# Attention of a transformer block: another order of turns, bias rows for each query tile side by side, and the high halves of the gated product on GpSimd

## The chip, the cores and the metric

The kernel runs on one core of a Trainium2 chip. The metric is the device time of one execution in microseconds. The program is one long instruction stream for each of the five engines: TensorE (PE, with its weight loads shown as PEld), VectorE (DVE), ScalarE (ACT), GpSimd (POOL) and SyncE (SP), which here only issues DMAs. The streams wait for each other through semaphores.

## What is computed

Two transformer blocks follow each other on 512 tokens of 1024 values: first an attention with a forget gate and a SwiGLU network, then a gated linear attention and a mixture of 64 experts. The change lies only in the first attention, the "fox" mixer. It has 16 heads of 64 values; 16 meta tokens stand ahead of the 512 real ones, and their outputs aren't needed.

```python
def _fox_attend(q_blk, c_q, pos_q, k, v, c_k, pos_k):
    s = jnp.einsum('bhqd,bhkd->bhqk', q_blk, k).astype(jnp.float32) * (FOX_HEAD_DIM ** -0.5)
    s = s + (c_q[..., :, None] - c_k[..., None, :])
    s = jnp.where(pos_k[None, :] <= pos_q[:, None], s, -jnp.inf)
    p = jax.nn.softmax(s, axis=-1)
    return jnp.einsum('bhqk,bhkd->bhqd', p, v.astype(jnp.float32))
...
    o = o * jax.nn.sigmoid(gate.astype(jnp.float32))
    return (o.astype(h.dtype) @ w_out).astype(h.dtype)
```

The term of the query, c_q, is the same for a whole row and falls out of the softmax. What stays is a bias for each key, -c_k, the same for all queries of a head, and the causal mask.

## The kernel before

Matrix products with weights are made from split values: a number is taken apart into a high half (a cast to fp32r) and a low half (the value minus its high half), and three products are summed. ACT casts the high halves, POOL subtracts to get the low ones.

The attention stage lies at about 215 to 330 us. The heads are taken in 8 pairs, and each pair in T = 4 query tiles of 128 queries. A step s = 4 p + i is query tile i of pair p; it has n = 16 + 128 (i + 1) keys, so 144, 272, 400 and 528. In each step, for both heads e of the pair:

- PE, `scores(s)`: the scores into PSUM, two steps ahead of the rest of its loop.
- DVE, `rowmax(s)`: adds the bias rows to the scores, writes the sum to SBUF (`Pb`, three buffers) and keeps the negated row maximum. Only the last 128 keys of a tile need the causal mask, so the keys are cut: the unmasked ones against the plain rows `cb`, the last 128 against the masked rows `cbm`; keys from 512 on have a cut of their own, since they lie in another PSUM bank. Each cut is two instructions for each head, the sum and the read of its accumulator.
- ACT, `exps(s)`: the exponential in place, and its row sum.
- DVE, `normed_probs(s)`: the reciprocal of the sums, and the product of the probabilities with it.
- PE, `ptrans(s)`: transposes the probabilities 128 columns at a time into two PSUM banks; ACT, `pt_out(s)`: copies them out.
- PE, `pv(p, half)`: the product with the values for query tiles 0 and 1 (half 0) or 2 and 3 (half 1). It starts with the 16 meta keys (tile `PTm`).
- DVE, `gated(p)`: the output of the pair times the gate, into the one buffer `prod_o`. Its high half is `hTh[p]` (`out_high`), its low half `hTl_first[p]` (`out_low`, POOL). `gated(p)` waits until `out_low(p-1)` has read `prod_o`, and `pv(p, 0)` until `gated(p-1)` has read its PSUM bank.

For the next pair POOL scales the queries and keys (`stage(p, 0)`, `stage(p, 1)`), PE transposes them (`qk(p, 0)` and `qk(p, 1)`, both through the one PSUM bank `QB`), and ACT evicts them to `QT` and `KT` (`qk_out`). The second transpose waits for the first eviction, and `scores` of the pair's first step wait for the second.

The bias rows of a pair come by DMA from `c_dram`, copied to all 128 partitions. `decay_rows(p)` issues them from SP; there are two places for them, so those of pair p wait for the last `rowmax` of pair p-2. POOL then makes the masked rows (`masked_rows(p)`), behind the two `stage` of pair p, and `rowmax` of the pair's first step waits for them. Each engine goes through all of this in the order of its written loop; nothing overtakes. At the end of the last pair, PE mixes the first sums of the output projection in (`early_sums`).

Of the kernel before, what the change touches and what calls it, by code (L numbers as in the profile page):

```python
# [48 lines left out]
def program(nc, x, meta_tokens, attn_norm, ffn_norm, final_norm, fox_w_in, fox_b_f, fox_q_norm, fox_k_norm,  # L49
# [32 lines left out]
    with ExitStack() as ctx:  # L82
# [85 lines left out]
        tail = W_SLOTS * 4096  # L168
        CB = L + SEQ - P
        cbs = [arena[:, 3712:3712 + 2 * CB], wring[:, tail:tail + 2 * CB]]  # L170
        cb = [[v[:, e * CB:e * CB + L] for e in range(2)] for v in cbs]
        cbm = [[v[:, e * CB + L:(e + 1) * CB] for e in range(2)] for v in cbs]
        Pb = [[wring[:, 4096 + (2 * i + e) * L:4096 + (2 * i + e + 1) * L] for e in range(2)] for i in range(3)]
# [3 lines left out]
        PT_last = [qkvg[:, :, e * D:e * D + 2 * P] for e in range(2)]  # L177
        at_ptm = at_pt + 2 * SEQ
        PTm = [wring[0:META, at_ptm + i * 4 * P:at_ptm + (i + 1) * 4 * P].rearrange("p (e q) -> p e q", e=2) for i in range(2)]
        assert at_ptm + 8 * P <= W_SLOTS * 4096 + CK_SLOTS * 1024  # L180
        gateT = [xn_t[:, p * SEQ:(p + 1) * SEQ] for p in range(PAIRS)]
# [492 lines left out]
        def _(sp):  # L674
            for t in range(T):
                sp.dma_start(xres[:, t, :], x[0, t * P:(t + 1) * P, :]).then_inc(s_x[t], 16)
            def decay_rows(p):

                if p >= 2:
                    sp.wait_ge(s_mx, 2 * T * (p - 1))  # L680
                for e in range(2):
                    h = 2 * p + e
                    sp.dma_start(cb[p % 2][e], c_dram[h:h + 1, :].to_broadcast([P, L])).then_inc(s_cb[p % 2], 16)

            for w, (slot, dmas, release) in enumerate(tiles):
                name = tile_names[w]
                if name == "g1":
                    sp.wait_ge(s_eD, evacs(unitsB, first_of["cm", 0]))
                    sp.dma_start(c_dram[:, :], cT).then_inc(s_cd, 16)
                elif name == "wo0":  # L690
                    sp.wait_ge(s_mB, first_of["f", 0] + 1)
                    sp.dma_start(gainrow[:, :], final_norm.rearrange("(a n) -> a n", a=1).to_broadcast([P, D])).then_inc(s_row, 16)
                    sp.wait_ge(s_cd, 16)
                    sp.wait_ge(s_hr, 3)
                    decay_rows(0)
                elif name == "wo1":
                    sp.wait_ge(*v1_done)
                    for p in range(1, PAIRS):
                        decay_rows(p)
# [73 lines left out]
        def _(act):  # L773
# [146 lines left out]
            for s in range(NS):  # L920
                p, i = divmod(s, T)
                if s + 1 < NS:
                    exps(s + 1)
                if i == 0 and p + 1 < PAIRS:
                    qk_out(p + 1, 0)
                if i == 1 and p:
                    out_high(p - 1)
                pt_out(s)
                if i == 0 and p + 1 < PAIRS:
                    qk_out(p + 1, 1)  # L930
                if p == PAIRS - 1 and i == 0:
                    high_half(act, attn_end)
                if p == PAIRS - 1 and i == 2:
                    high_half(act, attn_end + 1)
                    high_half(act, attn_end + 2)
            out_high(PAIRS - 1)

# [250 lines left out]
        def _(pe):  # L1188
# [247 lines left out]
            for s in range(NS):  # L1436
# [5 lines left out]
                elif i == 0 and p:  # L1442
                    pv(p - 1, 1)
                if i == 0 and p + 1 < PAIRS:
                    qk(p + 1, 0)
                ptrans(s)
                if i == 0 and p + 1 < PAIRS:
                    qk(p + 1, 1)
                if s >= NS - 2:
# [498 lines left out]
        def _(dve):  # L1948
# [113 lines left out]
            def rowmax(s):  # L2062

                p, i = divmod(s, T)
                n = META + P * (i + 1)
                cuts = ([(512, n)] if n > 512 else []) + [(0, n - P), (n - P, min(n, 512))]
                if i == 0:
                    dve.wait_ge(s_cb[p % 2], 32 * (p // 2 + 1))
                    dve.wait_ge(s_cbm, p + 1)
# [3 lines left out]
                for m, (a, b) in enumerate(cuts):  # L2073
                    for e in range(2):
                        x = 2 * s + e
                        d = P * i + a - (n - P)
                        bias = cb[p % 2][e][:, a:b] if a == 0 or i == T - 1 else cbm[p % 2][e][:, d:d + b - a]
                        last = m == len(cuts) - 1
# [30 lines left out]
            for s in range(NS):  # L2109
# [3 lines left out]
                normed_probs(s)  # L2113
                if i == 0 and p:
                    gated(p - 1)
# [505 lines left out]
        def _(pool):  # L2621
# [61 lines left out]
            def masked_rows(p):  # L2683

                pool.wait_ge(s_cb[p % 2], 32 * (p // 2 + 1))
                for e in range(2):
                    diag = cb[p % 2][e][:, META:L].rearrange("p (t s) -> p t s", t=T)
                    over3 = amask[:, :].unsqueeze(1).to_broadcast([P, T - 1, P])
                    pool.tensor_tensor(cbm[p % 2][e].rearrange("p (t s) -> p t s", t=T - 1), diag[:, 0:T - 1, :], over3, ALU.add)
                    last = pool.tensor_tensor(diag[:, T - 1, :], diag[:, T - 1, :], amask[:, :], ALU.add)  # L2690
                last.then_inc(s_cbm, 1)

            def out_low(p):
                pool.wait_ge(s_ohi, p + 1)
                pool.tensor_tensor(hTl_first[p], prod_o, hTh[p], ALU.subtract).then_inc(s_olo, 1)
# [109 lines left out]
```

## Time and profile before

| | us |
|---|---|
| median of 3 runs | 1462.0 (1460.33 to 1466.8) |
| time of the profiled execution | 1460.39 |
| its span, first to last instruction | 1458.6 |
| PE busy | 1385.2 (95%) |
| DVE busy | 532.5 (37%) |
| ACT busy | 524.5 (36%) |
| POOL busy | 476.3 (33%) |
| mean granted TensorE clock | 0.992 of full speed |

Busy times are over the whole program. Matmuls are pipelined and a row's duration holds the time in the pipeline, so the time from the start of one to the start of the next tells more than the duration of one. Time outside the span is 1.8 us. The attention stage is 115 us of the 1458.6; the last 500 us or so are the experts, whose weights are streamed in at about 419 GB/s.

### The profile page before, as it was taken

How to read it: one execution, taken by the hardware profiler on the slowest of the kernel's cores; microseconds unless marked ns; L12 is line 12 of the kernel's file. 1: busy time of each engine (PE TensorE's matmuls, PEld its weight loads, DVE VectorE, ACT ScalarE, POOL GpSimd, SP SyncE). 2: the span in 40 equal slices, each digit the busy share in tenths (PEclk: the TensorE clock that was granted, in tenths of full speed). 3: DMA queues.
4: the chain of work that ended last, by engine and by line, in shares of the span. 5: the costliest groups of instructions: out<-in, count | busy, mean ns of one | idle time of the engine just before them, and what ended most of it. 6: DMA issues, size and time to landing. Idle time of an engine off the chain costs nothing. (4 is left out here: it accounts for less than half of the span.)

```text
span 1458.6 us, 26900 instructions
## 1 busy us (share of the span) xinstructions
PE 1385.2 (95%) x11180; PEld 1037.7 (71%) x11180; DVE 532.5 (37%) x1383; ACT 524.5 (36%) x1096; POOL 476.3 (33%) x457
## 2 busy tenths in 40 slices
PE   7999998889999999999989999999999999888986
PEld 6788876567788888888867787776666665555553
DVE  3102118761312200212153613355464464444435
ACT  4325438772422222222246532333332222222222
POOL 5334546434544444444455755320000000000000
PEclk9999999999999999999999999999999999999999
DMA  5133221004232223330232131659999999999995
GB/s 187 65 111 115 88 72 47 31 16 147 84 102 71 87 87 115 116 115 15 101 124 97 58 116 59 238 196 390 403 418 420 419 420 419 420 419 420 419 419 208
DMA packets 83899, 286.49 MB, mean 196 GB/s; under 512 B 8764, under 2 KB 31456, under 8 KB 59200
## 3 DMA queue, kind: packets, MB, share of 16 engines
q1 hardware_dynamic: 83376, 283.60, 50.0%
q8 instruction: 91, 1.49, 0.4%
q0 software_dynamic: 288, 1.05, 0.2%
q14 instruction: 32, 0.26, 0.1%
q10 hardware_dynamic: 112, 0.09, 0.0%
HBM read 282.59 MB, written 2.13 MB: 195 GB/s over the span
## 5 line engine op out<-in xcount | busy, mean ns | idle before, releaser
L491 POOL TENSOR_TENSOR wring_halves<-wring,wring_halves 128x512 fp32r<-128x512 f32 x274 | 356.9, 1307 | 376.9 <-ACT wring_halves L486 375.1
L486 ACT CAST wring_halves<-wring 128x512 fp32r<-128x512 f32 x274 | 168.3, 621 | 433.4 <-PE ps L1207 416.6
L1205 PE MATMUL ps<-wring_halves,big_halves 128*128 128x512 f32 x612 | 241.5, 395 | 4.9 <-POOL wring_halves L491 3.8
L1205 PE MATMUL ps<-hT_halves,wring_halves 128*128 128x512 f32 x480 | 187.4, 390 | 2.4 <-DVE big_halves L1964 2.4
L1206 PE MATMUL ps<-big_halves,wring_halves 128*128 128x512 f32 x480 | 186.8, 389 | 0.0
L1207 PE MATMUL ps<-hT_halves,wring_halves 128*128 128x512 f32 x480 | 186.7, 389 | 0.0
L2654 POOL TENSOR_TENSOR rstd<-rstd,half 128x1 f32<-128x1 f32 (+1 forms) x21 | 13.6, 649 | 505.3 <-DVE rstd L2607 476.6
L1207 PE MATMUL ps<-wring_halves,hT_halves 128*128 128x512 f32 x436 | 170.6, 391 | 0.0
L1206 PE MATMUL ps<-wring_halves,hT_halves 128*128 128x512 f32 x436 | 170.6, 391 | 0.0
L1205 PEld LDWEIGHTS ps<-wring_halves,big_halves 128*128 128x128 f32 x612 | 115.4, 189 | 33.4 <-POOL wring_halves L491 7.3
L1725 PE MATMUL ps<-xn,fixed 128*128 128x512 f32 x256 | 120.0, 612 | 0.4 <-DVE fixed L2402 0.4
L1205 PEld LDWEIGHTS ps<-hT_halves,wring_halves 128*128 128x128 f32 x480 | 90.1, 188 | 22.7 <-POOL wring_halves L491 2.9
L1207 PEld LDWEIGHTS ps<-hT_halves,wring_halves 128*128 128x128 f32 x480 | 90.1, 188 | 18.8
L1206 PEld LDWEIGHTS ps<-big_halves,wring_halves 128*128 128x128 f32 x480 | 90.1, 188 | 18.6 <-issue 0.2
L2492 DVE COPY arena<-ps 32x256 f32<-32x256 f32 x128 | 54.3, 424 | 118.5 <-PE ps L1780 113.7
L1207 PEld LDWEIGHTS ps<-wring_halves,hT_halves 128*128 128x128 f32 x436 | 82.3, 189 | 17.5
L1206 PEld LDWEIGHTS ps<-wring_halves,hT_halves 128*128 128x128 f32 x436 | 82.5, 189 | 16.4
L2525 DVE TENSOR_TENSOR xres<-xres,ps 128x512 f32<-128x512 f32 x128 | 82.6, 684 | 21.1 <-PE ps L1806 18.3
L2145 DVE TENSOR_TENSOR arena<-arena,ps 128x512 f32<-128x512 f32 x22 | 15.1, 684 | 195.3 <-ACT arena L955 195.3
L1725 PEld LDWEIGHTS ps<-xn,fixed 128*128 128x128 f32 x256 | 46.5, 192 | 54.2 <-issue 52.4
L1752 PE MATMUL ps<-big,arena 128*32 128x128 f32 x2048 | 65.0, 276 | 10.1 <-DMA big<-in_moe_w_dram 9.6
L1094 ACT COPY arena<-ps 32x256 f32<-32x256 f32 x128 | 46.4, 362 | 62.6 <-PE ps L1780 61.7
(349 smaller groups left out, 1997.5 us busy)
## 6 DMA issues: line engine op xcount, KB each, us to landing
big<-in_moe_w_dram SPq DMA_DIRECT2D x90, 1024.0 KB, 25.4
wring<-in_moe_w_dram SPq DMA_DIRECT2D x70, 1024.0 KB, 25.5
wring<-in_ffn_w_in_dram SPq DMA_DIRECT2D x22, 1024.0 KB, 7.1
hT<-in_moe_w_dram SPq DMA_DIRECT2D x20, 1024.0 KB, 25.3
wring<-in_fox_w_in_dram SPq DMA_DIRECT2D x7, 2048.0 KB, 8.7
wring<-in_gla_w_in_dram SPq DMA_DIRECT2D x6, 2048.0 KB, 7.8
mkv<-in_moe_w_dram SPq DMA_DIRECT2D x12, 1024.0 KB, 26.2
wring<-in_ffn_w_out_dram SPq DMA_DIRECT2D x4, 2048.0 KB, 7.7
```

The source lines that it names most:

```text
L486: act.copy(hi, src).then_inc(s_hi, 1)
L491: pool.tensor_tensor(lo, src, hi, ALU.subtract).then_inc(s_lo, 1)
L1094: last = act.copy(rows[:, n * YG:(n + 1) * YG], bank(6 + j % 2)[n * C:(n + 1) * C, 0:YG])
L1205: pe.matmul(out, lhs[1], rhs[0], start=start, stop=False)
L1206: pe.matmul(out, lhs[0], rhs[1], start=False, stop=False)
L1207: return pe.matmul(out, lhs[0], rhs[0], start=False, stop=stop)
L1725: last = pe.matmul(bank(n), one_hots(g)[1][:, t, :], xn[:, t, n * 512:(n + 1) * 512], start=(t == 0), stop=(t == T - 1))
L1752: last = pe.matmul(o[i * C:(i + 1) * C, 0:2 * HG], xeT[:, k, r * C:(r + 1) * C], w[:, :, i // 2, :, i % 2], start=(k == 0), stop=(k == KD ...
L2145: dve.tensor_tensor(prod[f % 2], sg[f % 2], bank((2 * f + 1) % 8), ALU.mult).then_inc(s_hid, 1)
L2492: last = dve.tensor_copy(rows[:, n * YG:(n + 1) * YG], bank(6 + j % 2)[n * C:(n + 1) * C, 0:YG])
L2525: dve.tensor_tensor(d, d, bank(n), ALU.add).then_inc(done, 1)
L2654: rooted.inc(pool.tensor_tensor(v, v, half[0:v.shape[0], 0:v.shape[1]], ALU.pow))
```

## The change

Four things change.

1. The turns of PE and ACT. In a pair's loop, PE no longer puts the transpose of the next queries ahead of `ptrans` of tile 0 and that of the keys behind it; it puts the queries behind `ptrans` of tile 0 and the keys behind `ptrans` of tile 1. ACT evicts them behind `pt_out` of the same tiles.
2. The gated product of the pair before moves on DVE from behind `normed_probs` of tile 0 to behind that of tile 1, and its high half from ACT to POOL, right ahead of the low half (for the last pair it stays on ACT).
3. The bias rows lie in SBUF once for each query tile, 144 + 272 + 400 + 528 = 1344 columns a head where there were 528 and 384 masked ones. Each is a DMA of its own. POOL adds the mask to the last 128 columns of each in place, and `rowmax` no longer cuts a tile at its last 128 keys.
4. The rows' first place begins lower in `arena`, over values that the projection of the meta tokens reads. So `decay_rows(0)` now waits on SP until that projection is done, ahead of the load of the tile `wo0`, and `PTm` moves to `mkv`.

```diff
-        CB = L + SEQ - P
-        cbs = [arena[:, 3712:3712 + 2 * CB], wring[:, tail:tail + 2 * CB]]
-        cb = [[v[:, e * CB:e * CB + L] for e in range(2)] for v in cbs]
-        cbm = [[v[:, e * CB + L:(e + 1) * CB] for e in range(2)] for v in cbs]
+        KEYS = [META + P * (i + 1) for i in range(T)]
+        CB = sum(KEYS)
+        cbs = [arena[:, 3328:3328 + 2 * CB], wring[:, tail:tail + 2 * CB]]
+        cb = [[[v[:, e * CB + sum(KEYS[:i]):e * CB + sum(KEYS[:i + 1])] for i in range(T)] for e in range(2)] for v in cbs]
...
-        PTm = [wring[0:META, at_ptm + i * 4 * P:at_ptm + (i + 1) * 4 * P].rearrange("p (e q) -> p e q", e=2) for i in range(2)]
+        PTm = [mkv[0:META, i * 4 * P:(i + 1) * 4 * P].rearrange("p (e q) -> p e q", e=2) for i in range(2)]
...
                 for e in range(2):
                     h = 2 * p + e
-                    sp.dma_start(cb[p % 2][e], c_dram[h:h + 1, :].to_broadcast([P, L])).then_inc(s_cb[p % 2], 16)
+                    for i in range(T):
+                        sp.dma_start(cb[p % 2][e][i], c_dram[h:h + 1, 0:KEYS[i]].to_broadcast([P, KEYS[i]])).then_inc(s_cb[p % 2], 16)
...
                     sp.wait_ge(s_hr, 3)
+                    sp.wait_ge(s_mB, unit_of["v", 1, T] + 1)
                     decay_rows(0)
...
@@ ACT @@
                 if s + 1 < NS:
                     exps(s + 1)
-                if i == 0 and p + 1 < PAIRS:
-                    qk_out(p + 1, 0)
-                if i == 1 and p:
-                    out_high(p - 1)
                 pt_out(s)
-                if i == 0 and p + 1 < PAIRS:
-                    qk_out(p + 1, 1)
+                if i < 2 and p + 1 < PAIRS:
+                    qk_out(p + 1, i)
...
+            act.wait_ge(s_ohi, PAIRS - 1)
             out_high(PAIRS - 1)
...
@@ PE @@
-                if i == 0 and p + 1 < PAIRS:
-                    qk(p + 1, 0)
                 ptrans(s)
-                if i == 0 and p + 1 < PAIRS:
-                    qk(p + 1, 1)
+                if i < 2 and p + 1 < PAIRS:
+                    qk(p + 1, i)
...
@@ DVE @@
-                cuts = ([(512, n)] if n > 512 else []) + [(0, n - P), (n - P, min(n, 512))]
+                cuts = ([(512, n)] if n > 512 else []) + [(0, min(n, 512))]
...
-                        bias = cb[p % 2][e][:, a:b] if a == 0 or i == T - 1 else cbm[p % 2][e][:, d:d + b - a]
+                        bias = cb[p % 2][e][i][:, a:b]
...
                 normed_probs(s)
-                if i == 0 and p:
+                if i == 1 and p:
                     gated(p - 1)
...
@@ POOL @@
                 for e in range(2):
-                    diag = cb[p % 2][e][:, META:L].rearrange("p (t s) -> p t s", t=T)
-                    over3 = amask[:, :].unsqueeze(1).to_broadcast([P, T - 1, P])
-                    pool.tensor_tensor(cbm[p % 2][e].rearrange("p (t s) -> p t s", t=T - 1), diag[:, 0:T - 1, :], over3, ALU.add)
-                    last = pool.tensor_tensor(diag[:, T - 1, :], diag[:, T - 1, :], amask[:, :], ALU.add)
+                    for i in range(T):
+                        own = cb[p % 2][e][i][:, KEYS[i] - P:KEYS[i]]
+                        last = pool.tensor_tensor(own, own, amask[:, :], ALU.add)
...
             def out_low(p):
+                if p < PAIRS - 1:
+                    pool.wait_ge(s_prod, p + 1)
+                    pool.tensor_copy(hTh[p], prod_o).then_inc(s_ohi, 1)
```

On PE, in the loop of pair 1, from the end of `pv(0, 1)` (L1402) to the start of `pv(1, 0)` (L1399), the order before is this. L1352 is the transpose of queries or keys, L1380 and L1385 are `ptrans`, L1369 the scores.

```order
L1402 MATMUL ps<-big 64x128 x2
L1352 MATMUL ps<-ident,arena 128x128 x4
L1380 MATMUL ps<-ident,wring 128x128 x2
L1385 MATMUL ps<-ident,wring 16x128 x2
L1352 MATMUL ps<-ident,arena 128x128 x4
L1369 MATMUL ps<-arena 128x272 x2
L1369 MATMUL ps<-arena 128x240 x2
L1380 MATMUL ps<-ident,wring 128x128 x4
L1385 MATMUL ps<-ident,wring 16x128 x2
L1369 MATMUL ps<-arena 128x144 x2
L1399 MATMUL ps<-wring,mkv 64x256 x2
```

The same place of the changed kernel, where every line number on PE is lower by 2:

```order
L1400 MATMUL ps<-big 64x128 x2
L1378 MATMUL ps<-ident,wring 128x128 x2
L1383 MATMUL ps<-ident,wring 16x128 x2
L1350 MATMUL ps<-ident,arena 128x128 x4
L1367 MATMUL ps<-arena 128x272 x2
L1367 MATMUL ps<-arena 128x240 x2
L1378 MATMUL ps<-ident,wring 128x128 x4
L1383 MATMUL ps<-ident,wring 16x128 x2
L1350 MATMUL ps<-ident,arena 128x128 x4
L1367 MATMUL ps<-arena 128x144 x2
L1397 MATMUL ps<-mkv 64x256 x2
```

The first group of L1350 (queries) has gone behind `ptrans` of tile 0, the second (keys) behind the scores of tile 3 and `ptrans` of tile 1, right ahead of the next pair's first scores, which need the evicted keys.

On ACT, in the same stretch, the order before is this. L894 is `exps`, L907 and L908 are `pt_out`, L882 evicts the queries, L886 and L887 the keys, L913 is `out_high`.

```order
L882 ACTIVATE arena<-ps,gcol 128x512
L908 COPY wring<-ps 128x128
L907 COPY wring<-ps 16x2x128
L908 COPY wring<-ps 128x128
L886 COPY arena<-arena 128x16
L887 ACTIVATE arena<-ps,gcol 128x512
L894 ACTIVATE wring,fixed<-wring,fixed 128x400 x2
L913 CAST hT_halves<-wring 128x512
L908 COPY wring<-ps 128x2x128
L907 COPY wring<-ps 16x2x128
L908 COPY wring<-ps 128x2x128
```

And in the changed kernel (line numbers are higher by 1):

```order
L909 COPY wring<-ps 128x128
L908 COPY mkv<-ps 16x2x128
L909 COPY wring<-ps 128x128
L883 ACTIVATE arena<-ps,gcol 128x512
L895 ACTIVATE wring,fixed<-wring,fixed 128x400 x2
L909 COPY wring<-ps 128x2x128
L908 COPY mkv<-ps 16x2x128
L909 COPY wring<-ps 128x2x128
L887 COPY arena<-arena 128x16
L888 ACTIVATE arena<-ps,gcol 128x512
```

The cast has left ACT, and the two evictions stand behind the copies of tiles 0 and 1.

## Rows read from the trace of the kernel before

**Rows 1.** Page, first line: span.

```profile
span 1458.6 us, 26900 instructions
```

**Rows 2.** Windows: us, busy us (x) of PE, PEld, DVE, ACT, POOL; granted clock.

```profile
249.69:257.25 7.56, 7.56 (x70) 5.17 (x70) 5.37 (x24) 5.64 (x18) 6.79 (x13) 1.00 0.21 74
257.25:262.80 5.55, 4.04 (x32) 2.76 (x30) 4.91 (x26) 4.61 (x15) 0.76 (x1) 1.00 0.00 0
...
265.00:267.00 2.00, 2.00 (x13) 1.33 (x11) 1.19 (x2) 1.47 (x5) 1.89 (x5) 0.50 0.41 157
```

**Rows 3.** Timeline, PE and ACT, 257 to 263 us: start, us, instruction [idle before].

```profile
257.25 0.66 PE L1352 MATMUL ps<-ident,arena 128*128 128x128 f32 x4
...
257.64 0.25 PEld L1380 LDWEIGHTS ps<-ident,wring 128*128 128x128 f32 x2
...
257.95 0.69 ACT L882 ACTIVATE arena<-ps,gcol 128x512 f32<-128x512 f32 x1 [1.98 <-PE ps L1352]
...
258.78 0.63 PE L1352 MATMUL ps<-ident,arena 128*128 128x128 f32 x4 [0.43 <-ACT arena L882]
...
259.44 0.20 ACT L886 COPY arena<-arena 128x16 f32<-128x16 f32 x1 [0.25 <-PE ps L1352]
259.55 0.68 ACT L887 ACTIVATE arena<-ps,gcol 128x512 f32<-128x512 f32 x1
...
260.13 0.62 ACT L894 ACTIVATE wring<-wring,fixed 128x400 f32<-128x400 f32 x1
...
261.20 0.52 PE L1369 MATMUL ps<-arena 64*128 64x144 f32 x4
...
261.36 0.61 ACT L913 CAST hT_halves<-wring 128x512 fp32r<-128x512 f32 x1
...
261.87 0.37 ACT L908 COPY wring<-ps 128x256 f32<-128x256 f32 x1
...
262.39 0.36 ACT L908 COPY wring<-ps 128x256 f32<-128x256 f32 x1
...
262.80 0.65 PE L1399 MATMUL ps<-wring,mkv 16*64 16x256 f32 x4 [1.08 <-ACT wring L908]
```

**Rows 4.** Timeline of the last pair, 312 to 318 us.

```profile
312.96 0.69 DVE L2106 TENSOR_TENSOR wring<-ps,xn 128x512 f32<-128x512 f32 x1 [2.67 <-PE ps L1402]
...
313.97 0.61 ACT L486 CAST arena_halves<-wring 128x512 fp32r<-128x512 f32 x1
...
316.14 0.71 PE L1380 MATMUL ps<-ident,wring 128*128 128x128 f32 x4 [1.57 <-DVE wring L2100]
...
317.78 0.65 PE L1399 MATMUL ps<-wring,mkv 16*64 16x256 f32 x4 [0.72 <-ACT wring L908]
```

**Rows 5.** Timeline of the start: SP, POOL, DVE and PE, 215 to 227 us.

```profile
215.40 0.80 SPq L683 DMA_DIRECT2D wring<-c_dram  x2
...
219.60 1.00 POOL L2689 TENSOR_TENSOR wring<-wring,fixed 128x384 f32<-128x384 f32 x1 [9.10 <-DMA wring<-c_dram]
...
224.93 0.16 DVE L2080 CUSTOM_DVE_ANT_0 wring<-ps,wring 128x16 f32<-128x16 f32 x1
...
226.53 1.09 PE L1380 MATMUL ps<-ident,wring 128*128 128x128 f32 x8
```

**Rows 6.** DMA queues, 215 to 224 us: packets, MB, share of 16 engines.

```profile
q1 hardware_dynamic: 288, 0.54, 22.2%
```

**Rows 7.** Groups by shape, 213 to 325 us: POOL (busy us, mean ns | idle).

```profile
L2695 POOL TENSOR_TENSOR big_halves<-wring,hT_halves 128x512 fp32r<-128x512 f32 x7 | 8.9, 1272 | 36.5 <-ACT hT_halves L913 36.5
...
L2689 POOL TENSOR_TENSOR wring<-wring,fixed 128x384 f32<-128x384 f32 x8 | 8.1, 1007 | 9.4 <-DMA wring<-c_dram 9.3
...
L2690 POOL TENSOR_TENSOR wring<-wring,fixed 128x128 f32<-128x128 f32 x8 | 3.7, 461 | 0.0
```

**Rows 8.** Timeline: `normed_probs` of 400 columns, POOL busy, then POOL idle.

```profile
262.79 1.23 DVE L2100 TENSOR_SCALAR wring<-wring,fixed 128x400 f32<-128x400 f32 x2
...
318.54 0.77 DVE L2100 TENSOR_SCALAR wring<-wring,fixed 128x400 f32<-128x400 f32 x2
```

More of the change, by code:

```diff
@@ L177, in program @@
         PT_last = [qkvg[:, :, e * D:e * D + 2 * P] for e in range(2)]
-        at_ptm = at_pt + 2 * SEQ
-        PTm = [wring[0:META, at_ptm + i * 4 * P:at_ptm + (i + 1) * 4 * P].rearrange("p (e q) -> p e q", e=2) for i in range(2)]
-        assert at_ptm + 8 * P <= W_SLOTS * 4096 + CK_SLOTS * 1024
+        PTm = [mkv[0:META, i * 4 * P:(i + 1) * 4 * P].rearrange("p (e q) -> p e q", e=2) for i in range(2)]
+        assert at_pt + 2 * SEQ <= W_SLOTS * 4096 + CK_SLOTS * 1024 and 3328 + 2 * CB <= 6144
         gateT = [xn_t[:, p * SEQ:(p + 1) * SEQ] for p in range(PAIRS)]
@@ L2065, in rowmax @@
                 n = META + P * (i + 1)
-                cuts = ([(512, n)] if n > 512 else []) + [(0, n - P), (n - P, min(n, 512))]
+                cuts = ([(512, n)] if n > 512 else []) + [(0, min(n, 512))]
                 if i == 0:
-                    dve.wait_ge(s_cb[p % 2], 32 * (p // 2 + 1))
+                    dve.wait_ge(s_cb[p % 2], 128 * (p // 2 + 1))
                     dve.wait_ge(s_cbm, p + 1)
@@ L2075, in rowmax @@
                         x = 2 * s + e
-                        d = P * i + a - (n - P)
-                        bias = cb[p % 2][e][:, a:b] if a == 0 or i == T - 1 else cbm[p % 2][e][:, d:d + b - a]
+                        bias = cb[p % 2][e][i][:, a:b]
                         last = m == len(cuts) - 1
@@ L2683, in masked_rows @@
             def masked_rows(p):
-                pool.wait_ge(s_cb[p % 2], 32 * (p // 2 + 1))
+                pool.wait_ge(s_cb[p % 2], 128 * (p // 2 + 1))
                 for e in range(2):
-                    diag = cb[p % 2][e][:, META:L].rearrange("p (t s) -> p t s", t=T)
-                    over3 = amask[:, :].unsqueeze(1).to_broadcast([P, T - 1, P])
-                    pool.tensor_tensor(cbm[p % 2][e].rearrange("p (t s) -> p t s", t=T - 1), diag[:, 0:T - 1, :], over3, ALU.add)
-                    last = pool.tensor_tensor(diag[:, T - 1, :], diag[:, T - 1, :], amask[:, :], ALU.add)
+                    for i in range(T):
+                        own = cb[p % 2][e][i][:, KEYS[i] - P:KEYS[i]]
+                        last = pool.tensor_tensor(own, own, amask[:, :], ALU.add)
                 last.then_inc(s_cbm, 1)
             def out_low(p):
+                if p < PAIRS - 1:
+                    pool.wait_ge(s_prod, p + 1)
+                    pool.tensor_copy(hTh[p], prod_o).then_inc(s_ohi, 1)
                 pool.wait_ge(s_ohi, p + 1)
```

## The prediction

> **What bounds the kernel now.** I read the page first. Of a span of 1458.6 us [rows 1] the change touches only the 115 us of attention; what it wins or loses there moves everything behind it by the same amount, since the projections and the network after it follow on PE at once, and the experts' weight stream starts when its places come free behind them. So the question is what sets the length of one pair of heads.
>
> The windows answer that. A pair is best cut at two points: A runs from the start of pv(p-1, 0) to the end of pv(p-1, 1), B from there to the start of pv(p, 0). In A, 7.56 us, PE is busy for all of it. In B, 5.55 us, PE is busy for 4.04: it idles 1.51 us [rows 2]. ACT is busy for 10.25 of the 13.11 us of the pair, DVE for 10.28, POOL for 7.55. No engine is full over the whole pair; A is PE's, B is a chain. The timeline of B shows the chain [rows 3]: PE turns the queries at 257.25, ACT evicts them at 257.95, PE waits for that (0.43) and turns the keys at 258.78, ACT evicts these at 259.44 to 260.13, makes the exponentials of tile 2 until 261.36, the cast of the gated product until 261.87, the copies of tile 1 until 262.39 + 0.36 = 262.75, and at 262.80 PE starts pv(1, 0), after 1.08 us of idling. 1.08 + 0.43 is the 1.51. DVE's wait of two and more us for the gated product, of which the last pair's is the longest [rows 4], lies beside that chain and is no part of it, except in the last pair, where no queries or keys are turned.
>
> **The chain B after the change.** Each hop has a price in [rows 3].
> - ptrans of tile 0 comes first now: four transposes, 257.25 to 257.64: 0.39.
> - Turning the queries until ACT starts: 257.95 - 257.25 = 0.70.
> - Evicting them, until ACT's next: as for the keys, 260.13 - 259.55 = 0.58.
> - Exponentials of tile 2: 261.36 - 260.13 = 1.23. Their input, rowmax of tile 2, needs scores that PE finished ahead of pv, so it is there.
> - Copies of tile 1, right behind: 0.88 from 261.87 to 262.75, of which about 0.1 overlaps what follows on ACT, as the cast's 0.61 overlaps by 0.10: 0.79. PE has turned tile 1 by then: from the turn of the keys at 258.78 to the end of ptrans of tile 1 at 261.20 it took 2.42, so it is through at 0.39 + 2.42 = 2.81, the exponentials only at 0.39 + 0.70 + 0.58 + 1.23 = 2.90.
> - The keys' eviction, small copy and large: 259.55 + 0.68 - 259.44 = 0.79.
> - From ACT's end to PE: 258.78 - (257.95 + 0.69) = 0.14.
> - The first scores of the next pair, which now stand between: 0.52, and then pv(p, 0) at once.
>
> The sum is 0.39 + 0.70 + 0.58 + 1.23 + 0.79 + 0.79 + 0.14 + 0.52 = 5.14 us, against 5.55. The 0.51 of the cast and the second turn-round of the one bank (0.14 + 0.66 or so) leave the chain; ptrans of tile 0 (0.39) and the scores (0.52) enter it. PE's idle time does not vanish: it stands together now, about 1.1 us, ahead of the scores, waiting for the evicted keys. A doesn't change, since PE is full there. So a whole pair gains 0.41 us, and pairs 1 to 6 give 6 x 0.41 = 2.5 us. Pair 0 gains 0.1 at most: its B was shorter already, having no cast.
>
> **The last pair.** There DVE stood waiting for pv(6, 1) until 312.96 and only then made rowmax of tile 2 and the probabilities of tile 1, for which PE waited 1.57 us [rows 4]. With the gated product behind them, both are ready when PE comes. Then ACT sets the pace: the cast of the weights at 313.97 takes 0.51 to its next, exponentials 1.23, copies 0.88, hop 0.05: pv(7, 0) at 316.64 in place of 317.78 [rows 4]. Gain 1.1 us.
>
> **Moved at no cost.** Merging cuts takes 64 pairs of instructions off DVE; DVE is busy 10.28 of 13.11 us [rows 2] and is not on the chain, so I count nothing for or against it. The gated product moved by a step stays ahead of rowmax of tile 3 and is needed only by pv(p, 0), 5 us later. PTm is as before. On SP, decay_rows(0) and behind it the load of wo0 start later than they did. wo0 is first read in the last pair, at 313.97 [rows 4], some 100 us later. The rows of pair 0 come while the projections' last tile is still being made, and their masks stand on POOL behind that tile's low halves, as before.
>
> **POOL and the rows.** For each pair POOL now makes 8 masks of 128 columns, 8 x 0.46 = 3.7 us, in place of 2 x (1.01 + 0.46) = 2.9 [rows 7], and a cast of 128x512. No row shows a cast on POOL; from below it is 0.46, as the 128 columns take, from above 1.27, as the subtraction of two such inputs takes [rows 7]. I take 1.0, as it has one input and writes as much. POOL's load goes from 7.55 to at most 9.6 us of 12.7: still no bound.
>
> The rows are 8 DMAs of 128 packets, 1.38 MB, in place of 2, 0.54 MB. Before, two landed 219.60 - 215.40 = 4.2 us after the first was issued [rows 5]. The queue moved 288 packets at 22.2% of 16 engines in 9 us, 0.111 us of an engine each [rows 6]; 256 are 1.8 us over 16 engines, which leaves 2.4 us fixed. If bytes set the price, 1.38 MB is 2.55 x 1.8 = 4.5 us; if packets do, 1024 x 0.111 / 16 = 7.1. Issuing eight at 0.4 is 3.2 us and lies beside. So they land 6.9 to 9.5 us after the first issue. From pair 2 on there is room. The rows of pair p+1 are issued when rowmax of tile 3 of pair p-1 is done, 0.2 us (the reciprocal) ahead of normed_probs at 262.79, and needed one pair after the end of that normed_probs [rows 8]: 0.2 + 1.2 + 13.1 = 14.5 us, less 0.4 for the shorter pair. The masks take 3.7, so up to 10.4 us of landing are free.
>
> Pair 1 has no such room. Its rows can't be issued before 215.40, when the projections end. They land at 222.3 to 224.9, are masked at 226.0 to 228.6, and were needed at 224.93 [rows 5]. From there PE started ptrans of tile 3 after 1.6 us, at 226.53 [rows 5]; with two sums in place of four I take 1.2. That comes to 227.2 to 229.8: a loss of 0.7 to 3.3 us, once. I take 1.5, nearer to the price by bytes, as the packets get shorter with the bytes. The Trainium skill (DMA: Bandwidth & Descriptors, Anatomy of one DMA) gives a DMA a fixed part of about 2.0 us and then its bytes at 436 GB/s; by that page the rows would land 2.0 + 3.2 = 5.2 us after the issue, and the loss would be nothing. The rows here moved at 0.54 MB in 1.8 us, which is 300 GB/s, so the row is the slower, and I go by it.
>
> **Sum.** -2.5 (six pairs) - 0.1 - 1.1 (last pair) + 1.5 (rows of pair 1) = -2.2 us. The profiled execution took 1460.4 us, so 1458.2; the median of the runs shown stands 1.6 above it, so I say 1459.8. Ends of this case: the loss 0.7 to 3.3, the chain 0.2 us a pair either way, and stretches at half clock: between 265 and 267 us the granted clock was 0.50 [rows 2], the lower of its two levels, 1.2 of 2.4 GHz, with PE busy before; two us at that level cost about one, and a second such stretch stands a pair later. One or two more or fewer shift the time by 1 to 3 us. So -6 to +2, 1456 to 1464.
>
> **Rivals.**
> 1. PE is fed fully: all 1.51 us of idling go in seven pairs, and 1.1 in the last: -11.7, 1450. It needs the keys' eviction to be ready before PE asks. Against it: ACT's hops in series behind the queries' turn are longer than PE's work there. Chance 0.06.
> 2. Slower: rows land late in every pair. It decides at 10.4 us of landing and 0.4 of slack that DVE has there (1.6 - 1.2). At 14 us each of six pairs would be 3.2 us late, 19 in all, and pair 1 by 7.8 (215.4 + 14 + 3.7 + 1.2 - 226.5): with the gains +23, 1485. For it: 2.5 times the bytes, four times the packets, all reading one row of DRAM. Against: even the price by packets ends at 9.5. Chance 0.06.
> 3. POOL, now busier, slows DVE. Two normed_probs of 400 columns took 1.23 us with POOL busy and 0.77 with it idle [rows 8]. The 0.4 of slack by itself covers most of such a 0.46. If it all lay on the path and two steps more of each pair met POOL, it would be 8 x 2 x 0.46 = +7.4, with the rest of my sum +5, 1467. Chance 0.08. The Trainium skill (SBUF — State Buffer, Who interferes with whom) says that tensor_scalar in a two-port mode and GpSimd exclude each other for a whole instruction, which speaks against work moved to GpSimd; the rows agree in direction.
> 4. Nothing to be measured comes out: the new wait for the keys takes back what the cast gave, because hops overlap less than I add up, or pair 1 loses the whole 3.3: 0 to +2, 1463. Chance 0.22.
> My forecast has the remaining 0.58.
>
> **Numbers.** What a measurement of this kernel can tell from no change is 0.5%, 7.3 us. Forecast and rival 4 are within it. Faster than 1454.7 holds rival 1 and a thin edge of the forecast with the clock stretches gone: 0.10. Slower than 1469.3 holds rival 2 and part of rival 3: 0.08. Same: 0.82. The range takes in the forecast, rival 4 and most of rival 3, and reaches down to a forecast without any half-clock stretch: 1453 to 1466.
>
> **What would show it.** In the changed profile the wait of PE's pv for ACT's copies is gone, and a wait of 1.0 to 1.3 us stands ahead of each pair's first scores (L1367), ended by ACT's key eviction (L888). DVE's wait ahead of the gated product is gone or under 0.5. POOL waits for the rows of pair 1 until 222.3 to 224.9, and DVE for POOL right after. The period of a pair is 12.7. If DVE waits for POOL in later pairs, rival 2 holds; if PE waits for DVE ahead of ptrans, rival 3. Most likely to be wrong: the size of the landing, and a hop of the chain that overlaps otherwise.

## The result and the profile after

The change makes the kernel slower: 1471.22 us (median of four runs, 1469.6 to 1471.98) against 1461.16 of the kernel before (four runs, 1458.47 to 1466.8). The ratio is 1.0061, 95% interval 1.0045 to 1.0076. The profiled execution took 1471.9 us. Its page begins with these rows; the span was 1458.6 before [rows 1]:

```profile
span 1470.0 us, 26853 instructions
...
PE 1389.5 (95%) x11180; PEld 1042.3 (71%) x11180; DVE 521.9 (36%) x1255; ACT 521.6 (35%) x1089; POOL 485.2 (33%) x496
```

I measure attention from the start of pv(0, 0) to that of pv(7, 1). It took 326.79 - 223.33 = 103.46 us before and 335.88 - 223.41 = 112.47 now: +9.0 of the 11.4 us that the span grew. The windows of the trace after, over attention and over its first 23 us (columns as in [rows 2], then DMA share and GB/s):

```profile
216.00:335.90 119.90, 100.78 (x794) 70.69 (x794) 71.33 (x264) 80.11 (x248) 62.70 (x126) 0.93 0.34 82
223.00:246.00 23.00, 16.28 (x108) 10.76 (x108) 9.04 (x35) 10.95 (x34) 14.53 (x33) 0.78 0.31 88
```

The same stretch of attention in the trace before:

```profile
216.00:326.80 110.80, 98.13 (x794) 67.70 (x794) 81.53 (x392) 82.98 (x255) 52.91 (x86) 0.97 0.11 36
```

DVE's work fell from 81.5 to 71.3 us, as the merged cuts should make it, and the DMA share rose from 0.11 to 0.34. But in the first stretch PE idles 6.7 us of 23, and its granted clock is 0.78, so for part of it the clock is at the lower of its two levels. The timeline of that place shows why, to be read against [rows 5]:

```profile
215.43 5.08 SPq L683 DMA_DIRECT2D wring<-c_dram  x8
...
222.41 6.78 SPq L683 DMA_DIRECT2D arena<-c_dram  x8
...
227.37 3.33 POOL L2684 TENSOR_TENSOR wring<-wring,fixed 128x128 f32<-128x128 f32 x8 [9.87 <-DMA wring<-c_dram]
...
230.83 0.31 DVE L2075 CUSTOM_DVE_ANT_0 wring<-ps,wring 128x144 f32<-128x144 f32 x1 [7.57 <-POOL wring L2684]
...
232.12 1.97 PE L1378 MATMUL ps<-ident,wring 128*128 128x128 f32 x8 [5.56 <-DVE wring L2095]
...
236.32 1.11 PE L1397 MATMUL ps<-mkv 16*64 16x256 f32 x4
...
237.36 3.25 PE L1400 MATMUL ps<-big 128*64 128x256 f32 x16
```

The rows of pair 1 are issued at the same time as before, 215.4, but land at 227.37 in place of 219.60. Their masks end at 230.7, DVE starts 5.9 us later than at [rows 5], PE stands for 5.56 us, and then runs at half clock: eight transposes take 1.97 us where [rows 5] has 1.09, and sixteen matmuls of pv 3.25, where the trace before has 1.73. DVE's waits for POOL's masks come back in later pairs. The view of waits for 213 to 345 us (us in total, times, longest):

```profile
POOL wring L2684 <- DMA wring<-c_dram: 27.8, 4, 10.4
...
POOL arena L2684 <- DMA arena<-c_dram: 14.1, 3, 7.4
...
DVE wring L2075 <- POOL wring L2684: 9.7, 3, 7.6
...
PE ps L1378 <- DVE wring L2095: 9.5, 5, 5.6
...
PE ps L1367 <- ACT arena L888: 8.1, 7, 1.2
```

The last of them is the wait for the evicted keys, seven times 1.16 us: the one that the prediction named. Start by start, the 9.0 us are made up as follows (pv(p, 0) to pv(p, 1) is A less its last 2.24 us; pv(p, 1) to the next pair's pv is B with these):

| | before | after | difference |
|---|---|---|---|
| A of pair 1 | 5.45 | 12.91 | +7.5 |
| A of pairs 2 to 7 | 5.32 and twice 6.9 | 6.89, 5.48, 8.70, 5.32, 6.62, 5.93 | +3.9 |
| B behind A of pair 1 | 7.79 | 9.22 | +1.4 |
| five further B | 7.79 | 7.24, once 7.39 | -2.6 |
| B of the last pair | 7.18 | 6.05 | -1.1 |
| last pv pair | 9.01 | 9.00 | 0.0 |

So the chain gained somewhat more than was forecast (0.55 us a pair for 0.41), and A, which "doesn't change", lost 11.3.

### The profile page after: what moved, and what is told of

Its sections match the earlier page's. It is cut to its first block and busy times, and to the rows that moved or that the text cites. A ratio compares the mean times of both kernels' runs of the same rounds, so it can differ in the third digit from the quotient of the medians.

```text
span 1470.0 us, 26853 instructions
## 1 busy us (share of the span) xinstructions
PE 1389.5 (95%) x11180; PEld 1042.3 (71%) x11180; DVE 521.9 (36%) x1255; ACT 521.6 (35%) x1089; POOL 485.2 (33%) x496
## 5 line engine op out<-in xcount | busy, mean ns | idle before, releaser
L2487 DVE COPY arena<-ps 32x256 f32<-32x256 f32 x128 | 54.4, 425 | 119.5 <-PE ps L1776 114.9
```

The source lines that it names most:

```text
L2487: last = dve.tensor_copy(rows[:, n * YG:(n + 1) * YG], bank(6 + j % 2)[n * C:(n + 1) * C, 0:YG])
```

## Experiments

"Attention" in the table is the time from pv(0, 0) to pv(7, 1) in the profiled execution, "landing" the time from the first issue of pair 1's rows to POOL's first mask. The kernel before, on the chips of these runs, had medians of 1461.9 to 1462.9, and the ratios are to those. Each kernel has one trace, so its attention holds the stretches at the lower clock of that one execution; each costs about 1.6 us.

| kernel | time, us | ratio, 95% interval | attention | landing |
|---|---|---|---|---|
| before | 1461.2 | | 103.5 | 4.2 |
| after | 1471.2 | 1.0061 (1.0045 to 1.0076) | 112.5 | 11.9 |
| old_rows | 1457.7 | 0.9965 (0.9952 to 0.9979) | 98.9 | 4.1 |
| rows_only | 1474.4 | 1.0081 (1.0065 to 1.0096) | 114.9 | 12.3 |
| one_row | 1457.1 | 0.9957 (0.9940 to 0.9973) | 97.4 | 6.0 |
| split_rows | 1458.7, one run | | 97.8 | 6.9 |
| own_source | 1456.7 | 0.9954 (0.9936 to 0.9972) | 98.8 | 7.7 |
| same_source | 1467.7, one run | | 107.5 | 11.2 |
| prod_only | 1456.2 | 0.9957 (0.9942 to 0.9971) | 97.7 | 4.2 |
| turns_only | 1468.2 | 1.0032 (1.0017 to 1.0048) | 109.3 | 4.1 |
| keys_first | 1452.5 | 0.9919 (0.9897 to 0.9941) | 94.7 | 4.2 |
| keys_one_row | 1452.8 | 0.9929 (0.9908 to 0.9950) | 95.4 | 6.2 |

The times follow attention within about 2 us.

### Which part loses: old_rows and rows_only

My theory at this point: the order and the gated product gain some 4 us, the rows lose some 14.

**old_rows** is the changed kernel with the rows of before: one DMA a head, and masks, cuts and places as before.

```diff
-                    for i in range(T):
-                        sp.dma_start(cb[p % 2][e][i], c_dram[h:h + 1, 0:KEYS[i]].to_broadcast([P, KEYS[i]])).then_inc(s_cb[p % 2], 16)
+                    sp.dma_start(cb[p % 2][e], c_dram[h:h + 1, :].to_broadcast([P, L])).then_inc(s_cb[p % 2], 16)
```

> The kernel before with the new order of turns, the gated product moved and its high half on POOL, but with the old bias rows: one DMA of 528 columns a head, masked rows apart, rowmax cut as before. Theory 1 (the late rows are the whole loss): no wait of DVE for POOL, rows landed 4 to 5 us after their issue, a pair in 12.5 to 12.7 us where pv to pv took 13.1, the last pair 1.1 us shorter; 3 to 5 us less than the kernel before, ratio 0.997 to 0.998. Theory 2 (the turns themselves cost, and the late rows only add to it): at or above the kernel before, ratio 1.000 to 1.004.

1457.73 us, faster than before. No wait of DVE for POOL is left. Its timeline of one B, PE and ACT, answers to [rows 3]:

```profile
258.54 0.44 PE L1377 MATMUL ps<-ident,wring 128*128 128x128 f32 x2
...
259.03 0.60 PE L1349 MATMUL ps<-ident,arena 128*128 128x128 f32 x4
...
263.09 0.52 PE L1366 MATMUL ps<-arena 64*128 64x144 f32 x4 [1.15 <-ACT arena L887]
263.53 0.65 PE L1396 MATMUL ps<-wring,mkv 16*64 16x256 f32 x4
...
259.67 0.69 ACT L882 ACTIVATE arena<-ps,gcol 128x512 f32<-128x512 f32 x1
260.25 0.62 ACT L894 ACTIVATE wring<-wring,fixed 128x400 f32<-128x400 f32 x1
...
261.48 0.35 ACT L908 COPY wring<-ps 128x256 f32<-128x256 f32 x1
...
262.25 0.20 ACT L886 COPY arena<-arena 128x16 f32<-128x16 f32 x1
```

Each hop is within 0.1 us of the prediction: 0.49 for ptrans of tile 0 (0.39), 0.64 from the turn to ACT (0.70), 0.58 for the eviction, 1.23 for the exponentials, 0.77 for the copies (0.79), 0.84 from the keys' small copy to PE (0.79 + 0.14), 0.44 from the scores to pv (0.52). B is 5.00, from 258.54 to 263.53.

**rows_only** is the kernel before with the rows, masks, cuts and places of the change alone.

> The changed kernel with the old order of turns, the gated product and its high half where they were: of the change only the rows for each query tile are left. Theory 1: rows land 12 us after their issue as in the changed kernel, DVE waits 12 us or more in all for POOL's masks; where rows set the pair the better order was hidden, so the time is that of the changed kernel or up to 3 us above it: ratio 1.006 to 1.009 to the kernel before. Theory 2: rows cost only part, ratio 1.002 to 1.004.

1474.36 us: the rows alone cost more than the whole change. B is 7.79 again (from pv to pv), A of pair 1 takes 13.8 in place of 5.45. B behind pair 1, at 7.94, is the one exception. What loses is the rows.

### What makes the rows late: bytes, DMAs, or the source

After has more bytes (1.38 MB for 0.54), more DMAs and packets (8 and 1024 for 2 and 256), and, what rival 2 only mentions, four DMAs that all read the start of the same row of DRAM. The DMA view of the trace after, 215 to 228 us, in 40 slices of 0.33 us (GB/s), then the queue, then the issues with their own landing:

```profile
GB/s 183 151 44 0 43 48 48 44 50 93 96 95 100 123 125 141 118 87 100 178 148 195 173 234 295 201 199 229 171 151 178 267 164 162 230 274 198 195 196 152
...
q1 hardware_dynamic: 1614, 1.89, 66.4%
...
wring<-c_dram SPq DMA_DIRECT2D x2, 264.0 KB, 7.1
...
wring<-c_dram SPq DMA_DIRECT2D x2, 72.0 KB, 4.9
```

The rate begins at 45 to 50 GB/s, then about 95, then 125 and more. The rows of the four tiles have packets of 576, 1088, 1600 and 2112 bytes, and a DMA of 128 such packets in 1.45 us would be 51, 96, 141 and 186 GB/s. So the four DMAs of the first head seem to go one after another at one time each, whatever their size. From 222.4 us on the rows of pair 2 mix in, and the rate tells no more. The packets in the trace, told apart by their sizes, say the rest. Those of the first head end at 218.5, 220.1, 221.8 and 223.1 us. Those of the second head, which read another row, begin only at 222.3 and end at 223.9, 225.0, 226.2 and 227.0. From the first packet to the last the eight take 10.6 us, 1.3 us each. In pair 3, where nothing mixes in, they take 11.1. The reading of the rates came after the result, and the next kernels test it.

**one_row** writes the four tiles' rows side by side in DRAM (1344 columns a head) and fetches all with one DMA a head: the same bytes, masks and cuts as the change, in 256 packets.

```diff
-                    for i in range(T):
-                        sp.dma_start(cb[p % 2][e][i], c_dram[h:h + 1, 0:KEYS[i]].to_broadcast([P, KEYS[i]])).then_inc(s_cb[p % 2], 16)
+                    sp.dma_start(cbs[p % 2][:, e * CB:(e + 1) * CB], c_dram[h:h + 1, :].to_broadcast([P, CB])).then_inc(s_cb[p % 2], 16)
```

> The changed kernel, but the 1344 columns of a head lie side by side in DRAM (four small stores in place of one), so that one DMA a head brings them: same bytes, 256 packets of 5.4 KB for a pair in place of 1024 of 0.6 to 2.1 KB. If the number of packets or of DMAs sets the landing, the rows land 6 to 8 us after the issue, DVE waits for POOL only at pair 1, and the time is 1 to 4 us under the kernel before. If bytes set it, they land 11 to 13 us after the issue as before, and the time is that of the changed kernel.

1457.14 us. The rows land 6.0 us after the issue, and DVE waits for POOL 1.7 us in pair 1. Its timeline:

```profile
221.13 3.60 POOL L2684 TENSOR_TENSOR wring<-wring,fixed 128x128 f32<-128x128 f32 x8 [10.22 <-DMA wring<-c_dram]
...
224.87 0.31 DVE L2075 CUSTOM_DVE_ANT_0 wring<-ps,wring 128x144 f32<-128x144 f32 x1 [1.68 <-POOL wring L2684]
```

It isn't the bytes: the same 1.38 MB come in half the time. (One DMA a head also means fewer packets and no shared source, so this run by itself doesn't say which of the two counts.)

**split_rows** is old_rows with each row fetched in four DMAs of 132 columns: the bytes of before, the eight DMAs and 1024 packets of the change, each DMA with a source of its own.

```diff
-                    sp.dma_start(cb[p % 2][e], c_dram[h:h + 1, :].to_broadcast([P, L])).then_inc(s_cb[p % 2], 16)
+                    for a in range(0, L, L // 4):
+                        sp.dma_start(cb[p % 2][e][:, a:a + L // 4], c_dram[h:h + 1, a:a + L // 4].to_broadcast([P, L // 4])).then_inc(s_cb[p % 2], 16)
```

> As old_rows, but each row of 528 columns comes in four DMAs of 132: 8 DMAs and 1024 packets for a pair as in the changed kernel, with 0.54 MB in place of 1.38. If bytes set the landing, the rows land 4 to 6 us after the first issue; if packets or DMAs set it, 9 to 12 us. The masks are shorter here (2.9 us), so at 9 to 12 us only pair 1 is late.

**same_source** differs from it in one place: all four DMAs read columns 0 to 131. It leaves out the bias of the other columns, so only its times mean something.

```diff
-c_dram[h:h + 1, a:a + L // 4]
+c_dram[h:h + 1, 0:L // 4]
```

> split_rows, but all four DMAs of a head read columns 0 to 131, so the bias of the other columns is wrong: same 8 DMAs, 1024 packets and 0.54 MB for a pair. If DMAs that read the same DRAM addresses go one after the other, at about 1.5 us each as the changed kernel's, the rows land 11 to 13 us after the first issue in place of 6.9. If the addresses play no part, 6.9 again.

The timeline and the DMA view (215 to 228 us) of split_rows:

```profile
215.91 3.64 SPq L684 DMA_DIRECT2D wring<-c_dram  x8
...
222.81 0.99 POOL L2685 TENSOR_TENSOR wring<-wring,fixed 128x384 f32<-128x384 f32 x1 [11.83 <-DMA wring<-c_dram]
...
GB/s 0 0 0 0 0 15 47 41 57 63 52 55 76 154 152 98 185 185 85 177 151 57 39 0 50 0 0 0 0 15 47 46 47 83 78 111 156 115 151 151
```

and of same_source:

```profile
215.30 3.64 SPq L684 DMA_DIRECT2D wring<-c_dram  x8
...
226.53 0.99 POOL L2685 TENSOR_TENSOR wring<-wring,fixed 128x384 f32<-128x384 f32 x1 [16.13 <-DMA wring<-c_dram]
...
GB/s 0 0 0 8 45 39 49 44 42 49 44 46 42 49 39 44 47 59 28 20 39 47 68 255 200 62 47 78 76 70 89 55 85 112 80 29 47 46 41 44
```

Number, size and issue time of the DMAs are the same, only the addresses read differ. With its own source each, the rate climbs to 150 GB/s and more, and all have landed after 6.9 us. With one source a head it stays at 39 to 49 for the first 4 us, which is 67.6 KB (one DMA) in about 1.5 us, and the landing is 11.2. In attention that is 107.5 us against 97.8.

**own_source** asks the same of the changed kernel itself: its eight DMAs, packets, bytes, masks and cuts, but each tile's row is read from its own place in DRAM, side by side as in one_row.

```diff
-                        sp.dma_start(cb[p % 2][e][i], c_dram[h:h + 1, 0:KEYS[i]].to_broadcast([P, KEYS[i]])).then_inc(s_cb[p % 2], 16)
+                        sp.dma_start(cb[p % 2][e][i], c_dram[h:h + 1, sum(KEYS[:i]):sum(KEYS[:i + 1])].to_broadcast([P, KEYS[i]])).then_inc(s_cb[p % 2], 16)
```

> The changed kernel with the rows laid side by side in DRAM as in one_row, but brought by 8 DMAs a pair as in the change: same DMAs, same packet sizes and counts, same bytes; only that no two DMAs of a pair read the same addresses. If the many small packets or the 8 DMAs set the landing, the rows land 12 us after the first issue and the time is that of the changed kernel (ratio 1.005 to 1.008). If it is that the four DMAs of a head read the same DRAM addresses, they land 7 to 9 us after it and the ratio is 0.995 to 0.998.

1456.74 us, 14.5 below the changed kernel (the ratios 0.9954 and 1.0061). Its timeline and its DMA view (215 to 228 us):

```profile
215.49 3.73 SPq L683 DMA_DIRECT2D wring<-c_dram  x8
...
223.18 3.34 POOL L2685 TENSOR_TENSOR wring<-wring,fixed 128x128 f32<-128x128 f32 x8 [9.71 <-DMA wring<-c_dram]
...
GB/s 0 0 0 0 28 50 51 46 145 97 158 296 295 307 372 353 340 316 229 283 390 340 150 63 0 5 50 50 50 76 134 100 124 122 152 177 276 399 358 355
...
q1 hardware_dynamic: 1877, 2.17, 49.4%
```

More packets and bytes than in the same window of after, at a smaller share of the 16 engines. The rate passes 300 GB/s, and the landing is 7.7. A of pair 1 takes 6.84: the masks end at 226.52 and PE stands 1.33 us for what DVE makes of them. The six behind it take 5.32, but for one of 6.89 with a half-clock stretch. So the shared source is what takes the landing from 7.7 to 11.9 us. The 3.5 us from 4.2 to 7.7 come with the other bytes, packets and DMAs, and cost little: the wait of 1.33.

### What gains: prod_only and turns_only

**prod_only** is the kernel before with the gated product behind tile 1 and its cast on POOL; turns and rows are as before.

```diff
-                if i == 1 and p:
-                    out_high(p - 1)
...
-                if i == 0 and p:
+                if i == 1 and p:
                     gated(p - 1)
...
+                if p < PAIRS - 1:
+                    pool.wait_ge(s_prod, p + 1)
+                    pool.tensor_copy(hTh[p], prod_o).then_inc(s_ohi, 1)
```

> The kernel before, with its old order of turns and its old rows; only the gated product goes behind tile 1 on DVE and its high half to POOL. By the chain of B, the cast alone leaves it: 5.55 - 0.51 = 5.04 us a pair, and the last pair gains its 1.1: as good as old_rows, ratio 0.996 to 0.998. The rival, that the order of turns is what gains, gives B 5.5 and only the last pair's 1.1: 0.999.

1456.20 us. B is 5.04 in each pair (pv to pv 7.28 in place of 7.79), and the last pair's pv to pv is 6.05 in place of 7.18. This part has the whole gain of the change.

**turns_only** is the kernel before with the new order of turns and evictions, nothing else.

```diff
-                if i == 0 and p + 1 < PAIRS:
-                    qk(p + 1, 0)
                 ptrans(s)
-                if i == 0 and p + 1 < PAIRS:
-                    qk(p + 1, 1)
+                if i < 2 and p + 1 < PAIRS:
+                    qk(p + 1, i)
```

> The kernel before with only the order of turns changed: old rows, gated product behind tile 0 and its cast on ACT. By the chain, B is 5.0 + 0.51 = 5.5 us a pair, and DVE waits for the gated product as before: ratio 0.999 to 1.001. The rival, that the turns gain by themselves: B 5.0, ratio 0.997.

1468.21 us: slower than before, which I had not expected. B is 5.77 where I had 5.5. Its timeline, DVE and ACT, and a window of its last pair:

```profile
260.70 0.69 DVE L2102 TENSOR_TENSOR wring<-ps,xn 128x512 f32<-128x512 f32 x1 [1.69 <-PE ps L1400]
261.31 0.43 DVE L2076 CUSTOM_DVE_ANT_0 wring<-ps,wring 128x272 f32<-128x272 f32 x1
...
261.71 0.69 ACT L882 ACTIVATE arena<-ps,gcol 128x512 f32<-128x512 f32 x1
...
262.54 0.63 ACT L894 ACTIVATE wring<-wring,fixed 128x400 f32<-128x400 f32 x1
...
263.78 0.60 ACT L913 CAST hT_halves<-wring 128x512 fp32r<-128x512 f32 x1
...
323.53:328.00 4.47, 4.47 (x23) 3.13 (x24) 2.51 (x11) 2.43 (x7) 0.22 (x1) 0.62 0.00 0
```

DVE waits for pv(p-1, 1) and makes the gated product before rowmax of tile 2. With one eviction less ahead of them, the exponentials of tile 2 now come before their input is there: at 262.54, 0.25 later than right behind the queries' eviction, which takes 0.58 to the next instruction (261.71 + 0.58). The cast follows on ACT. So the new order needs the gated product moved. B is thus 0.2 us a pair longer than before, 1.6 in all, which doesn't make the 5.9 us of attention: A takes 6.89, 8.17 and 6.90 in three pairs, and the last pv pair 10.58 in place of 9.01, each with a stretch at half clock as in the last row (0.62). It is not one odd trace: over the twelve runs the mean granted clock was 0.987, over the 26 of the kernel before 0.990. Why this order brings more such stretches isn't shown.

### A better order: keys_first

In B the keys' eviction waits behind the copies of tile 1 on ACT, though PE needs it for the scores first. **keys_first** is old_rows with the keys turned ahead of ptrans of tile 1 and evicted ahead of its copies.

```diff
+                if i == 1 and p + 1 < PAIRS:
+                    qk(p + 1, 1)
                 ptrans(s)
-                if i < 2 and p + 1 < PAIRS:
-                    qk(p + 1, i)
+                if i == 0 and p + 1 < PAIRS:
+                    qk(p + 1, 0)
```

(the same for qk_out around pt_out on ACT)

> old_rows with the next keys turned by PE ahead of ptrans of tile 1 and evicted by ACT ahead of the copies of tile 1, so that the next pair's first scores run while ACT copies. By the chain the scores (0.5) leave B: 4.5 us in place of 5.0 a pair, PE's wait ahead of the scores goes from 1.2 to under 0.6, 3 us less than old_rows: ratio 0.994 to 0.996 to the kernel before. The rival, that PE then waits for the queries' eviction ahead of the keys: B 5.0, the time of old_rows.

1452.45 us, 9.5 below the kernel before. Timeline of one B:

```profile
258.38 0.68 ACT L887 ACTIVATE arena<-ps,gcol 128x512 f32<-128x512 f32 x1
...
259.11 0.52 PE L1368 MATMUL ps<-arena 64*128 64x144 f32 x4 [0.37 <-ACT arena L887]
...
259.88 0.65 PE L1398 MATMUL ps<-wring,mkv 16*64 16x256 f32 x4 [0.26 <-ACT wring L908]
```

The wait of 1.15 becomes 0.37 + 0.26, B is 4.54, and A is 5.32 in all seven pairs, with no stretch at half clock before the last. Of the 4.2 us of attention below old_rows, B makes 2.8 (0.46 in six pairs), as forecast; most of the rest is A of one pair, which in the trace of old_rows has such a stretch (6.88).

**keys_one_row** joins it with one_row, to see whether DVE's saved work is worth something once the rows are in time.

> The changed kernel with both mends: rows side by side in DRAM, one DMA a head (one_row), and the next keys turned and evicted ahead of tile 1 (keys_first). The rows for each tile take work only from DVE, which is not on the chain, and land 1.8 us later than the old ones, which pair 1 feels: 6.8 us from pv to pv in B as in keys_first, and the time of keys_first or up to 2 us above it, ratio 0.992 to 0.994. The rival, that DVE's saved work counts: 2 us or more under keys_first.

1452.76 us, the same. B is 6.78 from pv to pv in both, A of pair 1 is 6.07 for 5.32. DVE's busy time in attention falls from 79 to 69 us and brings nothing.

## Why the prediction was wrong

It said 1459.8, within 1453 to 1466, with 0.08 for slower. It came out at 1471.2. Rival 2, rows late in every pair, is what happened, though not in each of them.

**The step that failed** is the landing: "If bytes set the price ... 4.5 us; if packets do ... 7.1. ... So they land 6.9 to 9.5 us after the first issue." They took 11.9 in pair 1, and 11.9 to 12.8 in the others behind it. So the term of +1.5 us for pair 1 came out as 7.5. A of the later pairs, which stands in the sum at nothing, came out as 3.9. Both hold stretches at half clock. Both prices took a DMA's cost from the share of the 16 engines that [rows 6] shows, as if several DMAs would share them freely. The runs show a third price: eight such DMAs, four on each head's row, go one behind another at 1.3 to 1.4 us each; with a place of its own for each they overlap, and the eight take 6.2 us from the first packet to the last (own_source, pair 1). Rival 2 names "all reading one row of DRAM" as a reason and gives it no number.

The trace before already held a bound from above. Its DMA view, 215 to 228 us:

```profile
GB/s 0 0 0 0 78 201 162 195 208 299 279 240 26 0 0 0 0 0 0 0 0 0 0 0 50 0 0 0 0 32 175 169 175 247 325 254 202 78 7 0
```

The two DMAs of pair 1 move for nine slices of 0.33 us, 2.9 us in all and not 1.8, so one takes about 1.45. Eight at that price, one after another, are 11.6 us, beyond the range that I gave. The Trainium skill (DMA: Bandwidth & Descriptors, Anatomy of one DMA) gives the 2.0 us and 436 GB/s for a DMA on GpSimd's path, and SP issues those here. The 5.2 us that I worked out from it, an estimate, lie below all three landings of these bytes: 6.0 in one_row, 7.7 in own_source and 11.9 in the change. The 6.9 to 9.5 from my rows held for own_source, and so did the time (1456.7), but not for the change.

**The point of decision held.** I had 10.4 us of landing free, and 0.4 of slack. With landings of 11.9 to 12.8 that leaves 1.1 to 2.0 us a pair. DVE waited for POOL 7.57, 0.86, 2.51, 2.10 and 1.27 us, in five pairs of seven; after a wait the next rows are issued later too, and the pair behind it can be in time. With 7.7 (own_source) no wait is left behind pair 1. For pair 1 my formula gives 227.4 + 3.7 + 1.2 - 226.5 = 5.8, and PE idled 5.56; for own_source it gives 223.2 + 3.7 + 1.2 - 226.5 = 1.6, and PE idled 1.33.

**The chain B was right**: 5.14 foretold, 5.00 measured; PE's wait at the scores 1.15 (1.0 to 1.3 foretold). The last pair gained 1.13 (1.1). But prod_only shows that moving the product and its cast makes the whole of it. The order of turns, whose terms (0.39 and 0.52 in, 0.80 out) make the chain 0.11 us longer in my own sum, adds 0.04 of gain (5.04 to 5.00); without the product moved it loses (turns_only, 5.77 against 5.55).

**Left out: the half clock after a wait.** I let such stretches vary by 1 to 3 us. After PE's 5.56 us of idling the work behind ran at half clock, as above: that is the growth of B by 1.4 in place of a gain of 0.55, 2.0 us, and the 1.9 of the 7.5 of A that PE's wait doesn't cover. In rows_only and same_source, where PE waits 6.46 and 4.25 us in pair 1, the clock is down at the same place. The windows of after, rows_only and same_source:

```profile
231.00:236.00 5.00, 3.88 (x20) 3.16 (x22) 3.01 (x14) 2.94 (x10) 4.00 (x11) 0.50 0.32 82
231.00:236.00 5.00, 3.74 (x18) 3.01 (x20) 3.15 (x14) 2.81 (x10) 3.91 (x10) 0.50 0.37 93
231.00:236.00 5.00, 4.93 (x26) 3.72 (x26) 2.84 (x16) 2.51 (x8) 2.96 (x7) 0.50 0.15 25
```

In the other nine kernels, where PE waits 1.33 us or less there, it is at its full level. But other stretches came with no such wait, as the one of [rows 2]. The three slowest kernels have most of them: the mean granted clock over attention is 0.93 in after and turns_only and 0.94 in rows_only, but 0.97 before and 0.98 in keys_first, where only the last pair has such a stretch.

**POOL** was no bound. Its cast, which I put at 1.0 between 0.46 and 1.27, took 0.61. The trace after:

```profile
241.42 0.61 POOL L2690 CAST hT_halves<-wring 128x512 fp32r<-128x512 f32 x1 [3.02 <-DVE wring L2101]
```

Rival 3 would have to show in own_source, where POOL is as busy as in the change (61.7 us of the 112 from 213 to 325, after it 60.0). The normed_probs of 400 columns take 0.8 to 1.8 us there, but B is 7.24 from pv to pv, and A is 5.32 but for pair 1 and one stretch at half clock, as in old_rows with its 55.5 us of POOL: what DVE loses isn't on the path. DVE's saved work brought nothing, as I had it (keys_one_row against keys_first).

**Open.** Where in the path of reading the DMAs of one source queue up isn't shown; nor why the second head's DMAs, with a row of their own, begin only when the first head's are almost done; nor whether the half-clock stretches come from PE's waits or only go with them; nor the last 2.4 of the 11.4 us, which arise behind attention. There the trace after has four stretches at the lower clock and the trace before three; whether that is the 2.4 isn't shown.

## What to carry to other kernels

Before you split one broadcast load into several, ask whether they read the same addresses: here such DMAs queued up, from 528 to 2112 bytes a packet, and a copy side by side in DRAM, made once, took that away. One DMA for the whole copy landed sooner still (6.0 against 7.7 us). A load that now hides behind a pair needs its room worked out before its price, and a bound from above for each thing that is new about it. And sum an order of work hop by hop: the sum showed that the turns gain nothing and that the keys' eviction stood in the wrong place, which was worth another 2.8 us in B (1457.7 to 1452.5 in the whole, with a stretch at half clock fewer).

## What the runs showed of the hardware

- Eight broadcast DMAs of 128 packets, of which four at a time read the same place in DRAM, landed 11.2 us after the first issue where those with a place of their own took 6.9 (528 bytes a packet), and 11.9 where those took 7.7 (576 to 2112). Of the first four of them each took about 1.5 us, whatever its size.
- Issuing eight DMAs took SP 3.6 to 4.5 us in split_rows, own_source and same_source, but 5.1 to 6.8 in after and rows_only. A late landing alone doesn't explain it, since same_source lands as late; the cause isn't shown.
- A cast of 128x512 from f32 to fp32r on POOL takes 0.61 us, as on ACT (0.60), and half of a subtraction of two such inputs (1.27).
- PE's granted clock fell to its lower level at different pairs in different kernels with the same work, about 1.57 us each time (A 6.89 in place of 5.32).
